# Mod rows with the matrix moving, six load buffers for them, and low parts in place ahead of read-outs, in a differential-attention layer

## What is computed

```python
mod = silu(c) @ ada_w + ada_b                  # (3 * 2048,)
shift, scale, gate = split(mod, 3)
h = rms_norm(x, norm_pre) * (1 + scale) + shift
q, k, v, z = (h @ w_in[:, i*2048:(i+1)*2048] for i in range(4))
p = softmax(mask(q_m @ k_m.T * 128**-0.5))     # m = 0, 1, per head
o = (p[0] - lam * p[1]) @ v
o = rms_norm(o, subln) * (1 - lambda_init) * silu(z)
out = x + gate * rms_norm(o @ w_out, norm_post)
```

## Time and profile before

| | us |
|---|---|
| time, median of 3 runs | 2139.2 (2137.2 to 2139.2) |
| the profiled execution | 2142.9 |
| its span | 2141.1 |
| PE busy in the span | 2001.4 (93%) |
| DVE busy | 1276.9 (60%) |
| ACT busy | 783.8 (37%) |
| POOL busy | 578.6 (27%) |
| DMA queue q1, packets' time as a share of 16 engines | 63% |

### The profile page before, as it was taken

How to read it: one execution, slowest core, us unless ns; L and a number is a source line. 1 busy time by engine, 2 the same in 40 slices (tenths; PEclk the granted TensorE clock), 3 DMA queues, 4 the chain that set the end, 5 groups by cost and what they waited for, 6 DMA issues and landing times.

```text
span 2141.1 us, 26819 instructions
## 1 busy us (share of the span) xinstructions
PE 2001.4 (93%) x9444; PEld 1659.1 (77%) x9444; DVE 1276.9 (60%) x1996; ACT 783.8 (37%) x1563; POOL 578.6 (27%) x640
## 2 busy tenths in 40 slices
PE   3679999999999989899999999999999979999998
PEld 3668888888888868687787878788787868888886
DVE  3567666666566336577676767677676735434343
ACT  3233333333454323344343434444343424322241
POOL 1143333333456223232232323233142201000000
PEclk9989999999999999999999999999999989999999
DMA  8647666663556586576757676676766576466652
GB/s 266 215 136 246 215 198 219 199 190 128 181 179 229 195 311 216 173 225 197 215 184 226 196 208 210 194 220 190 228 189 199 184 258 198 126 189 199 200 158 79
DMA packets 390465, 426.53 MB, mean 199 GB/s; under 512 B 20054, under 2 KB 286396, under 8 KB 387772
## 3 DMA queue, kind: packets, MB, share of 16 engines
q1 hardware_dynamic: 390048, 424.76, 63.0%
q10 hardware_dynamic: 284, 0.05, 0.0%
HBM read 294.70 MB, written 130.03 MB: 198 GB/s over the span
## 4 chain that ended last, share of the span: by engine, by line
PE 85%; DVE 4%; DMA 4%; issue 3%; POOL 1%; SPq 1%; ACT 1%; DVEq 0%; POOLq 0%; ACTq 0%
PE ps L1522 27%; PE ps L1524 26%; PE ps L1523 26%; DMA q_dr<-ev 2%; PE ps L1627 1%; PE ps L1635 1%; DMA ada<-in_ada_w_dram 1%; PE ps L1605 1%; DVE acc L1111 1%; SPq L448 1%; POOL stg L713 1%; POOL sums L693 1%; DMA h_dr<-stg 1%; DVE blk L1138 1%; PE ps L1654 1%
## 5 line engine op out<-in xcount | busy, mean ns | idle before, releaser
L1522 PE MATMUL ps<-blk,ring 128*128 128x512 f32 x1536 | 612.2, 399 | 15.1 <-issue 7.6
L1524 PE MATMUL ps<-blk,ring 128*128 128x512 f32 x1536 | 600.7, 391 | 0.0
L1523 PE MATMUL ps<-blk,ring 128*128 128x512 f32 x1536 | 600.1, 391 | 0.0
L1522 PEld LDWEIGHTS ps<-blk,ring 128*128 128x128 f32 x1536 | 289.5, 188 | 75.7 <-issue 14.3
L1524 PEld LDWEIGHTS ps<-blk,ring 128*128 128x128 f32 x1536 | 289.3, 188 | 62.2
L1523 PEld LDWEIGHTS ps<-blk,ring 128*128 128x128 f32 x1536 | 289.9, 189 | 56.9
L1076 DVE TENSOR_TENSOR ring<-sums,ring 128x512 fp32r<-128x512 f32 x256 | 224.2, 876 | 130.5 <-ACT ring L796 128.4
L693 POOL TENSOR_TENSOR sums<-raw 128x512 f32<-128x512 f32 x128 | 192.6, 1505 | 316.4 <-DVE ring L1076 295.6
L796 ACT ACTIVATE ring<-sums 128x512 fp32r<-128x512 f32 x256 | 160.1, 626 | 192.8 <-PE ps L1524 187.4
L1076 DVE TENSOR_TENSOR ring<-raw,ring 128x512 fp32r<-128x512 f32 x192 | 161.7, 843 | 83.6 <-ACT ring L796 82.8
L693 POOL TENSOR_TENSOR sums<-sums,raw 128x512 f32<-128x512 f32 x128 | 186.0, 1453 | 26.1 <-DVE ring L1076 19.6
(11 more groups left out here) (156 smaller groups left out, 3158.3 us busy)
## 6 DMA issues: line engine op xcount, KB each, us to landing
raw<-in_diff_w_in_dram SPq DMA_DIRECT2D x64, 1024.0 KB, 7.0
ada<-in_ada_w_dram SPq DMA_DIRECT2D x128, 256.0 KB
d_dr<-cc SPq DMA_DIRECT2D x128, 256.0 KB, 2.7
cc<-d_dr SPq DMA_DIRECT2D x128, 256.0 KB, 3.7
w_raw<-in_diff_w_out_dram SPq DMA_DIRECT2D x128, 256.0 KB, 3.6
ada<-in_ada_w_dram SPq DMA_DIRECT2D x32, 512.0 KB
v_dr<-ev SPq DMA_DIRECT2D x64, 256.0 KB
q_dr<-ev SPq DMA_DIRECT2D x32, 512.0 KB
```

The lines of the kernel that those rows point to most:

```text
L1522: MM(dst, a_hi, b_hi, start=start, stop=False, skip_group_check=True)
L1523: MM(dst, a_hi, b_lo, start=False, stop=False, skip_group_check=True)
L1524: return MM(dst, a_lo, b_hi, start=False, stop=stop, skip_group_check=True)
```

## The change

1. Mod rows. Four slots of a chunk (1, 4, 6, 7) go to PE, with a column of cact stationary and 512 columns of ada moving, so that the sum is one row of 512 in one partition; `ada_sum` is one matmul. ACT copies the row to mod_row, and `mod_turn` makes four columns of it with four matmuls of one column. Two more load buffers (ada_more) lie on raw[1]; the second load of raw weights therefore waits for the slots in them.
2. DVE's order in a slot of the second half is `weights`, `posts`, `take`.
3. The low part is written over the block in its cc buffer (cc_low), and ev holds four high parts, one for each block of a group, which wait for the store of the group before. A cc buffer is free when the stores have landed; its next load is issued two slots behind the store. The cc buffers are given out anew: C22 always has the same one, the other four go round. Stores of q and k are two DMAs of 256 KB instead of one of 512 KB.
4. The first four loads of w_out and one load of oz stand ahead of the last `load_z` and `store_oz`.

```diff
-    ON_PE = (1, 4, 7)
+    ON_PE = (1, 4, 6, 7)
+    ADA_RING = 6
...
+        ada_more = at("ada_more", [P, ADA_RING - 4, 2, AC], F32, [base[0] - (ADA_RING - 4) * 2 * AC * 4])
...
+        cc_low = at("cc_low", [P, CCR, HALF], F32R, [cc_at[0]])
+        mod_row = at("mod_row", [P, AC], F32, [cc_at[0]])
...
-        ev = at("ev", [P, 2, 2, HALF], F32R, z_at)
+        ev = at("ev", [P, 4, HALF], F32R, z_at)
...
+        TURNS = (0, 4, 3, 1)
+
         def buffer_of(i, b):
-            return (4 * i + b) % CCR
+            return 2 if b == C22 else TURNS[(i + {C11: 0, C12: -1, C21: 2}[b]) % 4]
...
+            def load_ada_start(s):
+
+                ch, r = s // 8, s % 8
+                if s >= ADA_RING:
+                    sp.wait_ge(*slots_of(s - ADA_RING))
+                src = ada_v[:, 2 * r:2 * r + 2]
+                for m in range(2):
+                    sp.dma_start(ada_start(s)[:, :, m * 256:(m + 1) * 256],
+                                 src[:, :, m * D + ch * 256:m * D + (ch + 1) * 256]).then_inc(ada0_in[s % ADA_RING], 16)
...
             def load_partial(i, b):
 
-                buf, n = buffer_of(i, b), 4 * i + b
-                if n - CCR < 4 * GP:
-                    sp.wait_ge(d_st[buf], 16 * ((n - CCR) // CCR + 1))
-                else:
-                    sp.wait_ge(*left((n - CCR) // 4, ORDER.index((n - CCR) % 4)))
...
+                buf, old = buffer_of(i, b), before_in[i, b]
+                if old[0] < GP:
+                    sp.wait_ge(d_st[buf], 16 * uses[old])
+                else:
+                    sp.wait_ge(*stored_block(*old))
...
             for s in range(4 * 8):
-                load_ada(s)
-                if s in (15, 23):
-                    load_raw(s // 8 - 1)
+                load_ada_start(s)
+                if s == 15:
+                    load_raw(0)
+            sp.wait_ge(*slots_of(28))
+            sp.wait_ge(*slots_of(29))
+            load_raw(1)
...
                 for w in (n - 3, n - 2):
                     if w >= NA and w % NP in BLOCK and w == n - 1 - lag(w):
-                        f, fp = divmod(w, NP)
-                        store(f, fp)
-                        nxt = 4 * f + BLOCK[fp] + CCR
-                        if nxt < 8 * GP:
-                            load_partial(nxt // 4, nxt % 4)
+                        store(*divmod(w, NP))
+                for w in (n - 5, n - 4):
+                    if w >= NA and w % NP in BLOCK and w == n - 3 - lag(w):
+                        f, b = w // NP, BLOCK[w % NP]
+                        nxt = {C11: (f + 1, C12), C12: (f + 1, C21), C22: (f + 1, C22), C21: (f + 2, C11)}[b]
...
+                        if nxt[0] < 2 * GP:
+                            load_partial(*nxt)
...
                         slot(n)
                         n += 1
+                    if a + 1 == LH * NB:
+                        for j in range(4):
+                            load_wo(j)
+                        load_oz_first(1, 0)
                     load_z(h - 1, qb)
...
-            for j in range(4):
-                load_wo(j)
-            load_oz_first(1, 0)
...
+                act.wait_ge(ada_used, len(ON_PE) * (j + 1))
+                A(mod_row[0:1, :], ps[0:1, SC + j % 2], ACT.Copy).then_inc(mod_row_ok, 1)
                 for q in range(4):
                     modulate(4 * j + q)
...
-                e, x = o % 2, 4 * (i - GP) + o
-                if x >= 2:
-                    act.wait_ge(stored[e], 32 * (x // 2))
+                if i > GP:
+                    act.wait_ge(stored[o], 32 * (i - GP))
...
-                dve.wait_ge(ada_used, len(ON_PE) * (ch + 1))
+                dve.wait_ge(mod_turned, ch + 1)
...
                 for which in range(4):
                     block_sums(ch, tA, which)
+                if ch < 3:
+                    rows0(8 * ch + 11)
...
                 if ch < 3:
-                    for r in (3, 5, 6):
-                        rows0(8 * ch + 8 + r)
+                    rows0(8 * ch + 13)
...
                 if part == 0:
-                    i = STT(ev[:, e, 1], src, QKSCALE, ev[:, e, 0].bitcast(F32), ALU.mult, ALU.subtract)
+                    i = STT(cc_low[:, buf], cc[:, buf], QKSCALE, ev[:, o].bitcast(F32), ALU.mult, ALU.subtract)
...
                         weights(n)
                         if i == 0 and a:
                             out_scale(*before(a))
+                        posts(n)
                         if i == 1 and qb >= HT:
                             combine(h - 1, qb)
                         take(n)
                         if i == 0 and qb < HT:
                             combine(h - 1, qb)
-                        posts(n)
                         n += 1
...
+                for g in (2 * r, 2 * r + 1):
+                    i = MM(ps[0:1, SC + ch % 2], cact[:, g:g + 1], ada_start(s)[:, g % 2],
+                           start=g == 2 * ON_PE[0], stop=g == TG - 1)
+                i.then_inc(ada_used, 1)
...
+            def ada_sum(ch):
+
+                pe.wait_ge(row_ok, 8 * ch + 8)
+                MM(ps[0:1, SC + ch % 2], ones[:, 0:1], acc0[:, ch % 2], start=False, stop=False)
+
+            def mod_turn(ch):
+
+                pe.wait_ge(mod_row_ok, ch + 1)
+                if ch:
                     pe.wait_ge(mod_ok, ch)
...
                 for b in range(4):
...
+                    i = MM(ps[:, SC + 2, b:b + 1], mod_row[0:1, b * P:(b + 1) * P], ones[0:1, 0:1], start=True, stop=True)
+                i.then_inc(mod_turned, 1)
```

More of the change, by code:

```diff
@@ L226, in build @@
         ada_in = [sem(f"ada_in{i}") for i in range(4)]
-        ada_used, row_ok = sem("ada_used"), sem("row_ok")
+        ada0_in = [sem(f"ada0_in{i}") for i in range(ADA_RING)]
+        ada_used, row_ok, mod_row_ok = sem("ada_used"), sem("row_ok"), sem("mod_row_ok")
+        mod_turned = sem("mod_turned")
         consts = sem("consts")
@@ L245, in build @@
         post_hi, post_d, post_p, vt_mm = sem("post_hi"), sem("post_d"), sem("post_p"), sem("vt_mm")
-        stored = [sem("stored0"), sem("stored1")]
+        stored = [sem(f"stored{i}") for i in range(4)]
         q_ld, k_ld, z_ld = sem("q_ld"), sem("k_ld"), sem("z_ld")
@@ L320, in slots_of, with ada_start, stored_block @@
             return (ada_used, n) if s % 8 in ON_PE else (row_ok, 2 * (s + 1 - n))
+        def ada_start(s):
+            return ada[:, s % ADA_RING] if s % ADA_RING < 4 else ada_more[:, s % ADA_RING - 4]
         def lag(n):
             return 2 if head_part(n // NP)[1] == 2 else 1
+        TURNS = (0, 4, 3, 1)
         def buffer_of(i, b):
-            return (4 * i + b) % CCR
+            return 2 if b == C22 else TURNS[(i + {C11: 0, C12: -1, C21: 2}[b]) % 4]
+        used, uses, before_in = [0] * CCR, {}, {}
+        held = [None] * CCR
+        for i in range(2 * GP):
+            for b in (C11, C12, C22, C21):
+                buf = buffer_of(i, b)
+                used[buf] += 1
+                uses[i, b], before_in[i, b], held[buf] = used[buf], held[buf], (i, b)
+        loads = {n: uses[n] - max(uses[m] for m in uses if m[0] < GP and buffer_of(*m) == buffer_of(*n))
+                 for n in uses if n[0] >= GP}
+        def stored_block(i, b):
+            return stored[ORDER.index(b)], 32 * (i - GP + 1)
         def bank_done(G, t):
@@ L383, in store @@
                 m, half = (0, 0, 1, 1)[b], (0, 1, 1, 0)[b]
-                e = o % 2
+                buf = buffer_of(i, b)
                 tok = slice(half * HALF, (half + 1) * HALF)
                 sp.wait_ge(*split_done(i, o))
[L387 to L393, removed]
-                else:
-                    n = h * 4 + m * 2
-                    sp.dma_start((q_dr, k_dr)[part][n:n + 2, :, tok].rearrange("s p n -> p s n"),
-                                 ev[:, e].bitcast(F32)).then_inc(stored[e], 32)
+                if part == 3:
+                    sp.dma_start(z_dr[h * 2 + m, :, tok], cc[:, buf]).then_inc(stored[o], 32)
+                    return
+                for s, src in enumerate((ev[:, o], cc_low[:, buf])):
+                    if part == 2:
+                        dst = v_dr[h * SEQ + half * HALF:h * SEQ + (half + 1) * HALF].rearrange("(t p) s d -> p t s d", p=P)
+                        sp.dma_start(dst[:, :, s, m * P:(m + 1) * P],
+                                     src.rearrange("p (t d) -> p t d", t=HT).bitcast(F32)).then_inc(stored[o], 16)
+                    else:
+                        sp.dma_start((q_dr, k_dr)[part][h * 4 + m * 2 + s, :, tok], src.bitcast(F32)).then_inc(stored[o], 16)
             def load_qk(h, qb):
@@ L402, in load_qk @@
                 if qb == 0:
-                    for e in range(2):
-                        sp.wait_ge(stored[e], (h * 8 + 6) * 32)
+                    for e in range(4):
+                        sp.wait_ge(stored[e], (h * 4 + 3) * 32)
                 if a > 0:
@@ L416, in load_v @@
                 if qb == 0:
-                    for e in range(2):
```

(17 more changed lines are left out.)

68 lines of the change are left out of this document (29 added, 39 removed).

## The result

The changed kernel takes 2068.3 us (median of 4 runs, 2068.0 to 2068.6); the kernel before, run beside it, 2139.2 (2137.2 to 2144.6). The ratio is 0.967, with a 95% interval of 0.966 to 0.969: 71 us less, where 50 were predicted. The profiled execution took 2068.5 us with a span of 2066.7, so 74.4 us of span are to be found again.

What follows compares the result with a forecast made beforehand. The prediction took TensorE as the bound, with time to be had from the head and TensorE's gaps. Its terms, 13 + 28 + 0 + 2 + 7 = 50 us, took the median from 2139.2 to 2089 us, range 2066 to 2116.

Steps and rivals of the forecast that it cites:

- the first M: Head: end of the first chunk's mod columns, claimed at about 47 us at full clock, 54.8 at half.
- the cycles: Head, per chunk of mod rows: claimed 19.4 to 22.8 us instead of 26.0, the last 23.1 to 26.5.
- the choice between the bounds: Head: gain 3 us at half clock or 21 at full; 13 taken, expecting part at the upper level.
- nearly without gaps: Head: TensorE was claimed to have almost no idle time in a cycle, most of it 512-column work.
- its read-outs lose nothing behind the posts: Mixed stage: read-outs moved behind posts have 2.8 us to spare; read-out, weight and post take 2.1 on VectorE.
- the 1.4 us counted: Mixed stage: of at most 9 us lost to the clock, 1.4 claimed to fall with the gaps.
- seven late reloads of C22: Mixed stage, behind V groups: C22 claimed to land one microsecond late, seven times.
- The stop at the change of halves: At 786 us TensorE stands 5.9 us for a partial; claimed gain 2 us, 0 to 5.
- (a): Head: clock stays at the lower level throughout, gain 3 us instead of 13, time 2099; chance 0.20.
- all along: Head: claim, from durations, that it runs at the lower clock level (1.2 GHz) throughout, despite the printed clock.
- (b): Partials come late, stalling each group: whole gain gone from 5.7 us landings, 2173 us at 6.7; chance 0.08.
- (c): Mixed stage: V wait only changes place, to the product after next; 22 us less gain, 2111 to 2117; chance 0.10.

Runs made afterwards that it cites:

- matrix_stationary: Changed kernel with the mod matmuls in the old form, eight one-column matmuls a slot, without copy and turn: 2066.2 us.
- order_alone: Kernel before with only VectorE's new order (weights, posts, read-out), two high buffers and old stores kept: 2109.8 us.
- inplace_alone: Kernel before with only low parts in place, four high buffers and the new reload order: 2126.8 us.
- form_and_slot3: Changed kernel with the old one-column mod matmuls, no copy or turn, and slot 3 also on TensorE: 2073.1 us.
- reload_late: Changed kernel with each reload of a partial one slot later, three behind the store instead of two: 2091.8 us.
- slots3_5_on_pe: Changed kernel with slots 3 and 5 of each chunk also on TensorE, six there and two on VectorE: 2053.5 us.

## Why the prediction was right, and where it was short

The direction and the range held, and parts 1, 2 and 4 worked by the mechanisms named; 21 us of the gain were missing from the sum, nearly all of them from part 3 and from what parts 2 and 3 do for each other. By its steps:

- **Part 1 (13 us, bounds 3 and 21).** Right in its parts: a slot is 1.9 us, the turn 1.05 (0.95 reckoned), the first M comes at 46.6 (47), the cycles are 19.7, 20.5 and 24.4 (19.4 to 22.8 and 23.1 to 26.5), the wait from M to the first product stays. Run alone the part gives 14.3 us. Between the two traces of before and after the first product moves by 18.6; between the means of all five traces with the old head (131.4 to 135.5) and the four with the new one (116.7 to 118.2) it moves by 16.3. Mis-sized was the choice between the bounds: the middle was taken for the clock's sake. The first M came at the upper level's time; from a sum to M it took 6.5, 7.5 and 7.1 us (4.9 to 8.3), since slot 7 behind the idle piece ran mostly at the lower level; and from M to a sum 13.2, 13.1 and 17.4 us, where 14.5 and 18.2 were reckoned. Wrong was that TensorE would be nearly without gaps: 18.9 us of waits for VectorE are left. Slot 3's 1.6 us did become 3.43 beside GpSimd, but VectorE's work as a whole took less than reckoned; the waits follow from the prediction's own terms, since three slots and the transposes at the upper level are 7.7 us against VectorE's 14.5. The gain put down to the new form came without it in matrix_stationary; in that the 13 was lucky.
- **Part 2 (28 us).** Alone 27.3, and without it the 26.6 us wait is back to the tenth. That 27.3 stands so near 28 is partly luck, for two errors offset each other. The step that its read-outs lose nothing behind the posts held only with four high buffers: order_alone has 5.7 us more of aT_lo waits, so from 860 to 1650 its idle time fell by 17.3 us, not by the 23.7 of V waits there. And the clock was worth more than the 1.4 us counted: 10.6 us of it were lost in that stretch, 3.6 in order_alone.
- **Part 3 (0, a gain of 8 to a loss of 20).** This is the step that failed. Alone it gives 10.2 us, and on top of part 2 25.6 (52.9 - 27.3). The sum set 8 us of aT_lo waits against seven late reloads of C22. The reloads are late as reckoned, but VectorE's slack absorbs them, so no loss stood against the gain. And each part was costed against the kernel before: that part 2 would lengthen the wait for high parts, from 14.0 to 29.6 us, and that part 3 takes this away (4.5 with both), wasn't seen.
- **Part 4 (2 and 7 us).** The stop at the change of halves went from 5.90 to 4.36, that of the hand-over from 8.65 to 2.07: 1.5 and 6.6. Alone, the later loads give 5.2.
- **The rivals.** (a) fell: the clock rose in the head. The record that shows it is the first slot of the changed kernel, 2.24 us at 36.1 and 1.88 from 38.2 on, right behind 3.68 us of transposes, ahead of which TensorE had stood for 21.9. The rule on transposes in the Trainium skill, "TensorE: Matmul & The Clock Gate", Part 4, is not what this case shows: in matrix_stationary the slots behind the transposes take 2.29, 2.10 and 1.84 us and those ahead of them 3.5. The rise isn't the new form's alone, nor sure: with the old head the first two slots took 6.83 us in the trace of before and 4.05 and 4.00 in those of order_alone and inplace_alone, and one slot behind transposes in form_and_slot3 took 3.41. So the lower level "all along" was true of the trace that the prediction had, not of every run. (b) fell by reload_late; its error was to let every group stall by the whole lateness. (c) fell: no product waits in place of a V transpose, and the time isn't near 2111.

By the four parts alone plus the 15 us of parts 2 and 3 together, 57.0 + 15.4 = 72.4 us are found, against 71 measured. Of the 15.4, the stretch from 860 to 1650 shows about 10: its idle time falls by 30.7 us with both parts and by 6.8 and 17.3 with each alone, its lost clock by 10.6 against 0 and 7.0. Where the rest lies isn't shown.

## What to carry to other kernels

Parts of a change that touch one queue are costed against the kernel with the other parts in it: moving a wait forward in an in-order queue pays only when what it waits for comes free early enough. Where gaps of TensorE go, count the granted clock that was lost around them as well, from windows of 20 us, not from one rounded mean. When an engine is relieved in a cycle, lay its new order of work beside that of the engine it slows down, before calling the other engine the bound.

## What the runs showed of the hardware

- A f32 matmul with 512 moving columns and one stationary column is two records, 0.86 us together at the upper clock level and 1.71 at the lower (a slot of four records 1.72 to 1.88 and 3.4 to 3.6).
- In form_and_slot3 (60 to 80 us) TensorE was busy for 19.39 of 20 us, mostly with one-column matmuls, at a granted clock of 0.59; in slots3_5_on_pe, mostly with 512-column matmuls, for 16.94 of 20 us at 1.00. Behind sixteen transposes the next one-column slot was faster in three cycles of matrix_stationary (3.5 us ahead; 2.29, 2.10 and 1.84 behind), but 3.41 us in one cycle of form_and_slot3.
- The printed clock of the head of before was 1.00 from 40 to 100 us while durations showed the lower level; in the changed kernel, too, it prints 1.00 from 20 to 40 us, though the transposes at 32.5 take 3.68 us there and 1.97 at 54.
- Two multiply-adds of 128 x 512 on VectorE took 1.53 us with GpSimd idle and 3.43 beside its low parts (third cycle of the changed kernel's head); four low parts 2.48 and 6.75.
